# Output weights kept by column halves, one half tile of the projection moved ahead, and one weight piece asked for at its end

## The reference

```
u = rmsnorm(x); z = u @ w_in
a = pooling mixer(z[:, :512]); s = bidirectional S5 scan + GLU(z[:, 512:])
h = x + concat([a, s]) @ w_out
v = rmsnorm(h)
h = h + MoE(v)      # top 1 of 4 groups, then top 2 of its 8 experts, 32 experts of 1024 x 256 (gate, up, down)
h = h + sigmoid(rmsnorm(h) @ W_g + b_g) * (p @ W_ple)
out = rmsnorm(h)
```

## Time and profile before

| what | before |
|---|---|
| median of 3 runs | 522.41 us (522.15 to 522.5) |
| profiled execution, span from first to last instruction | 522.6 us |
| TensorE matmul busy | 484.2 us, 93% |
| VectorE, ScalarE, GpSimd busy | 238.9, 163.6, 161.0 us |
| DMA, mean over the span | 281 GB/s, 146.83 MB |

### The profile page before, as it was taken

The page is one execution under the profiler, slowest core; times in us unless marked ns, Lnnn a source line. Parts: engine busy times, 40 slices in busy tenths (PEclk is TensorE's granted clock), DMA queues, the critical chain, the costliest instruction groups (busy, mean ns, idle before and its releaser), DMA issues.

```text
span 522.6 us, 7298 instructions
## 1 busy us (share of the span) xinstructions
PE 484.2 (93%) x2744; PEld 273.3 (52%) x2744; DVE 238.9 (46%) x683; ACT 163.6 (31%) x265; POOL 161.0 (31%) x144
## 2 busy tenths in 40 slices
PE   3799999999999998999999999779999998899993
PEld 3446776634854476765555554435454544444441
DVE  2899987999233347653222222102211211474524
ACT  5643335456442344111111111002212121313464
POOL 1069999944100111132222222202120210003350
PEclk9999999999999989999999999879999998999998
DMA  8874200499289965999999999999999997970012
GB/s 298 141 204 88 62 0 2 159 129 208 108 360 422 415 249 192 407 412 423 418 415 419 417 419 409 423 416 421 418 420 420 419 409 296 345 312 0 0 80 80
DMA packets 57083, 146.83 MB, mean 281 GB/s; under 512 B 27602, under 2 KB 32758, under 8 KB 44248
## 3 DMA queue, kind: packets, MB, share of 16 engines
q1 hardware_dynamic: 50872, 133.92, 69.0%
q0 software_dynamic: 5904, 12.41, 6.1%
q10 hardware_dynamic: 272, 0.04, 0.0%
HBM read 138.17 MB, written 16.29 MB: 296 GB/s over the span
## 4 chain that ended last, share of the span: by engine, by line
PE 70%; DMA 18%; DVE 3%; ACT 3%; SPq 3%; issue 1%; DVEq 0%
PE bank L1586 65%; DMA h<-in_exp_w_up_dram 11%; DMA big<-in_exp_w_up_dram 6%; SPq L356 3%; DMA h<-in_x_dram 1%; PE bank L1935 1%; PE bank L1677 1%; PE bank L1954 1%; ACT L539 1%; ACT moe L531 1%; PE bank L1821 1%; PE bank L2052 1%; DVE ring L855 1%; DVE moe L1092 1%; DVE moe L855 1%
## 5 line engine op out<-in xcount | busy, mean ns | idle before, releaser
L1586 PE MATMUL bank<-ring,moe 128*64 128x256 f32 (+3 forms) x976 | 127.3, 385 | 3.4 <-DMA ring<-in_exp_w_up_dram 3.0
L1586 PEld LDWEIGHTS bank<-ring,moe 128*64 128x64 f32 (+1 forms) x976 | 76.2, 144 | 38.2 <-issue 15.3
L1512 POOL DMA_INDIRECT pairs_d<-moe,sidx_all x32 | 32.0, 1000 | 159.8 <-PE bank L1935 83.0
L855 DVE TENSOR_TENSOR vrow<-moe,bank 64x128 f32<-64x128 f32 x64 | 18.6, 291 | 125.5 <-ACT moe L754 120.6
L1586 PE MATMUL bank<-big,ut 128*128 128x512 f32 x128 | 58.2, 609 | 1.2 <-ACT ut L676 1.2
L1586 PE MATMUL bank<-ut,big 128*128 128x512 f32 x128 | 57.3, 596 | 1.8 <-ACT ut L543 1.8
L754 ACT ACTIVATE moe<-bank 64x256 f32<-64x256 f32 x32 | 12.1, 378 | 143.3 <-PE bank L1586 143.3
L1586 PE MATMUL bank<-ring,ut 128*128 128x512 f32 x128 | 55.7, 593 | 0.4 <-DVE ut L855 0.4
L531 ACT ACTIVATE moe<-bank 128x512 f32<-128x512 f32 x56 | 32.6, 598 | 59.8 <-PE bank L1586 49.3
L1586 PE MATMUL bank<-big,moe 128*64 128x256 f32 (+1 forms) x264 | 44.9, 455 | 6.6 <-DMA big<-in_exp_w_up_dram 5.7
L1586 PEld LDWEIGHTS bank<-big,ut 128*128 128x128 f32 x128 | 24.6, 196 | 32.0 <-issue 31.7
(11 more groups left out here) (193 smaller groups left out, 600.5 us busy)
## 6 DMA issues: line engine op xcount, KB each, us to landing
ring<-in_exp_w_up_dram SPq DMA_DIRECT2D x19, 1024.0 KB
ring<-in_exp_w_down_dram SPq DMA_DIRECT2D x18, 1024.0 KB
ring<-in_exp_w_gate_dram SPq DMA_DIRECT2D x17, 1024.0 KB
big<-in_exp_w_gate_dram SPq DMA_DIRECT2D x7, 1024.0 KB
big<-in_exp_w_down_dram SPq DMA_DIRECT2D x7, 1024.0 KB
big<-in_exp_w_up_dram SPq DMA_DIRECT2D x6, 1024.0 KB
ut<-in_exp_w_gate_dram SPq DMA_DIRECT2D x4, 1024.0 KB
h<-in_exp_w_up_dram SPq DMA_DIRECT2D x4, 1024.0 KB
```

Of the source, the lines that this page charges most:

```text
L855: return dve.tensor_tensor(o, a, b, op)
L1512: pool.indirect_dma_start(pairs, bass.IndirectOffsetOnAxis(ap=index, axis=0), at(moe, ALL, M_Y + k * 512, [[1, 512]]), None, bounds_check= ...
L1586: return pe.matmul(o, a, b, start=start, stop=stop, skip_group_check=loose)
```

## The change

w_out's rows 512 to 1023 are loaded by two DMAs, one for each half of the columns, each into one piece's place; the matmuls of `wout` read chunk c at `4 * DM + half * PIECE + (c - 4) * 512`. On TensorE `wout1(6)` moves from behind the logits of tiles 1 and 2 to a place ahead of tile 2's transposes, and on VectorE `residual(6)` moves from the middle of the routing arithmetic to a place ahead of tile 2's scaling. Since the add of half tile 6 no longer stands behind the reading of tile 1's logits, TensorE gets a wait of its own (`logit_sb`) ahead of the last tile's transposes, which go into the bank that held them. SyncE asks for piece 14 after seven half tiles, in place of eight; pieces 15 and 21 still wait for eight.

```diff
             sp.wait_ge(zp_ps, NB)
-            sp.dma_start(at(big, ALL, 4 * DM, [[DM, 4], [1, DM]]),
-                         dr(A["w_out"], 4 * P * DM, [[DM, P], [P * DM, 4], [1, DM]])).then_inc(ld_wout1, 16)
+            for half in range(2):
+                sp.dma_start(at(big, ALL, 4 * DM + half * PIECE, [[512, 4], [1, 512]]),
+                             dr(A["w_out"], 4 * P * DM + half * 512, [[DM, P], [P * DM, 4], [1, 512]])
+                             ).then_inc(ld_wout1, 16)
...
+            sp.wait_ge(wo1_ps, 2 * NT - 1)
+            weights(sp, 14)
             sp.wait_ge(wo1_ps, 2 * NT)
-            for p in (14, 15, 21):
+            for p in (15, 21):
                 weights(sp, p)
...
             logits(0)
+            residual(6)
             turned(2)
             norm(2)
             logits(1)
...
             first_best("sel", "m1", "q1", "q2", "oh1")
-            residual(6)
             seq(pick(qv("s2", eight), qv("oh1", eight), -3.0e38, qv("sel", eight), ALU.mult, ALU.add))
...
+                    w = c * DM + half * 512 if c < 4 else 4 * DM + half * PIECE + (c - 4) * 512
                     last = mm(bank[dst][:, :], at(ut, ALL, c * T + t * P, [[1, P]]),
-                              at(big, ALL, c * DM + half * 512, [[1, 512]]), c == chunks[0], c == chunks[-1])
+                              at(big, ALL, w, [[1, 512]]), c == chunks[0], c == chunks[-1])
...
-            pe.wait_ge(ld_wout1, 16)
+            pe.wait_ge(ld_wout1, 32)
...
             logits(0)
+            wout1(6)
             turned(2)
             logits(1)
             logits(2)
-            wout1(6)
             wout1(7)
+            pe.wait_ge(logit_sb, 2)
             turned(NA)
             logits(NA)
```

## The result

The change made the kernel slower: 524.92 us median of 8 runs (523.99 to 526.72) against 522.45 us (522.03 to 524.05, 8 runs), a ratio of 1.0037 with an interval of 1.0019 to 1.0055. The forecast was 520.4 us, with a range of 518.8 to 522.8 and a chance of 0.12 for slower.

What follows compares the result with a forecast made beforehand. Expert-weight transfers were taken to bound the kernel, with standstills before 304.8 us costing time at the end. The least of 2.5, 2.35 and 2.1 us, said as 2.0, off 522.41 gave 520.4 us, range 518.8 to 522.8.

Steps and rivals of the forecast that it cites:

- Step 3, d: VectorE's routing arithmetic and add of half tile 7: the whole routing chain comes 0.67 us later, the change's cost.
- Step 7, c: Experts' releases: pieces 24 to 26 have a lead of 2.8 us, so 2.1 us of gain stays after the delay.
- step 4: TensorE's clock may fall in `wout1(7)`, which then ends at 200.7, before VectorE's 201.36, so the chain does not move.
- slower: TensorE in the last tile's chain, 200.5 to 213 us: clock falls cost 1.7 us each, two give 523.7; chance 0.12.
- what bounds the kernel: Weight stream: a standstill before 304.8 us costs as much at the end; TensorE or VectorE time there costs nothing by itself.
- list of leads: Queue's stock over its next issue: 0.5 us for pieces 18 and 19, 2.8 for 24 to 26, 3.3 for the next.
- Step 2, a: SyncE's piece 14, issued at 190.95, moves before or in the dead stretch; at most 2.5 us leave the later queue.
- Step 6, b: Last h store lands earlier, pieces 18 and 19 go out at 209.65; the queue can be 2.35 us ahead without a gap.
- The lag of 1.0 us: Weight queue: 1.0 us from a DMA's issue to its first bytes; the forecast's own range allowed 1.0 to 1.7.
- Steps 1 and 5: Column halves of w_out cost nothing; tile 2's later scaling and store and the `logit_sb` wait make nothing wait.
- Hidden anyway: Weight queue: the gap only moves from 195 to behind 206 us, time stays about 522.3; chance 0.26.
- More than the piece: Last expert on TensorE: its clock stays up, saving some 1.6 us more, 518.8 us; chance 0.12.

Runs made afterwards that it cites:

- g0: The changed kernel run again with no edit; 524.79 us, one run.
- e4: The changed kernel with piece 14 asked for together with 15 and 21 again, so only the new order and halves remain; 525.22 us, ratio 1.0036.
- e1: The changed kernel with two 512-column matmuls of constants put into TensorE's wait for the masks; 523.88 us, ratio 1.0011 to the kernel before.
- g2: The changed kernel with two filler matmuls ahead of `rank(0)` and piece 18 early as well; 524.11 us, ratio 1.0014 to the kernel before.
- e3: The kernel before with column halves and piece 14 after seven half tiles, in the old order; 522.38 us, ratio 0.9991.
- e2: The kernel before with w_out's second half loaded by column halves and nothing else; 522.69 us, ratio 0.9988.
- g1: The kernel before with column halves and pieces 14 and 18 early, old order, second run of this edit; 523.69 us, ratio 1.0004.
- g3: The kernel before with column halves and piece 14 after seven half tiles, old order, second run of this edit; 523.17 us, ratio 0.9993.
- f1: The kernel before with two 512-column matmuls of constants ahead of `rank(0)`, a delay of 1.7 us; 523.78 us, ratio 1.0012.
- f2: The kernel before with four 512-column matmuls of constants ahead of `rank(0)`, a delay of 3.4 us; 525.15 us, ratio 1.0023.
- f0: The kernel before run once more, unedited, for a second profile; 522.58 us, one run.
- f3: The kernel before with column halves and pieces 14 and 18 early, old order, first run of this edit; 522.9 us, ratio 0.9978.

## Why the prediction was wrong

Two steps failed: step 3 priced the delay of the routing chain at 0.67 us, where it is 2.2, and step 7 took 2.8 us of such a delay to be free, where much less is. A fall of TensorE's clock, which step 4 and the rival "slower" had seen coming, came on top in after.

**Step 3, d: failed.** The working set the new order (201.36, measured 201.44) against 200.69 of the profile of before. That 200.69 holds a clock fall which six of the nine profiles of the old order don't have. The fall makes VectorE wait 2.21 us for half tile 6 in the middle of its arithmetic, and the forecast took wait and add together, 197.93 less 195.16 = 2.77 us, as what the move removes. Without a fall they are 0.58 and 0.61 (195.33 to 195.94), 1.2 us. Removing 1.2 from a delay of 3.44 leaves 2.2, as the table has it. The absolute times were right; the base was an execution of about 524.4 us that was set equal to a median of 522.41. Its span of 522.6, so near the median, hid this. By itself this step doesn't turn the sign: with d = 2.2 the forecast's own sum still has c = 2.8 - 2.2 = 0.6 us of gain.

**Step 4 and the rival "slower": the place was right, the weight too small.** In g0 the fall came in `wout1(7)`, where step 4 puts it, and there it is free. In after and e4 it came behind the wait for the masks, at the place that the rival names: 1.65 us in the chain of after (26.69 less 25.04), against its 1.7, and next to nothing in e4. e1 has neither the wait nor a fall, and is 1.3 us faster than e4. All three profiles of the new order without added matmuls have a fall somewhere, and three of the nine of the old; that is too few to say that the order makes falls more frequent. By the Trainium skill (TensorE: Matmul & The Clock Gate, HAM oscillation) falls follow idle gaps of TensorE. The traces agree in part only: with the gap filled the clock was up in e1 and g2, but at 192 it falls in some executions and in others not, with TensorE busy in all. The rival asked for two falls to turn the sign. With d = 2.2 and one fall, 3.9 us, the sum gives c = -1.1: a loss of 1.1 us, where 1.9 were measured (1.0037, 1.0 to 2.9).

**Step 7, c, and "what bounds the kernel": failed.** The step took a delay of the experts' releases to be free up to 2.8 us. The cleanest case against it has no delay at all: e3 was 2.2 us ahead and had lost all but 0.6 of it by 244 us, in part at the very issue with the lead of 2.8 (below). Of the delays, e1 and g2 have 2.2 us and no fall. e1's ratio is 0.0023 above e2's, 1.2 us; g2's is 0.0010 and 0.0021 above those of g1 and g3, 0.5 and 1.1 us. f1 and f2, with 1.7 and 3.4 us, are 0.6 and 1.2 us above the kernel before. The last expert's start says more: 1.5 and 1.6 us for e1 and g2, counted from tile 2's store and against f0. So between a quarter and three quarters of these 2.2 us reach the end, and the size of the lead is known only roughly: above nothing by f2's time, under 2.8 us by e1 and e3. The premise that TensorE's time ahead of 304.8 costs nothing by itself holds only for what the queue's stock covers, and that was overrated.

**What the list of leads leaves out.** Pieces 16 and 17 wait for the first picked rows, and 22 and 23 for an expert, so they hang on the same chain; the forecast has a lead for 18 and 19 and for 24 to 26, and none for these four. In after 16 and 17 go out at 215.74 us, 1.6 later than before (214.15), and the window from 216 to 217 moves 90 GB/s. From 208 to 226 us after's stream moves 326 GB/s and e3's 379, 1.0 MB or 2.3 us apart (after's whole stretch runs 0.6 us later than e3's, which is part of it), mostly before pieces 24 to 26 are asked for:

```profile
208.00:226.00 18.00, 16.62 (x135) 11.90 (x133) 12.59 (x48) 3.72 (x9) 3.58 (x4) 1.00 0.96 379
```

**Step 2, a: right in time, wrong in worth.** The piece filled the dead stretch (300 GB/s in 192 to 195 in after; 0.9 MB, 2.2 us, ahead of e2 at 208 us in e3). Then it was given back at two places. Windows of e3, and of g3 from 226 on microsecond by microsecond:

```profile
209.00:212.00 3.00, 3.00 (x28) 2.73 (x28) 2.27 (x7) 1.04 (x2) 0.00 (x0) 1.00 0.76 258
226.00:229.00 3.00, 2.56 (x24) 1.96 (x24) 1.06 (x2) 0.01 (x1) 1.87 (x3) 1.00 0.82 294
229.00:240.00 11.00, 11.00 (x84) 6.19 (x81) 3.04 (x8) 1.95 (x4) 3.33 (x5) 1.00 1.01 418
```

```profile
226.00:227.00 1.00, 0.96 (x8) 0.85 (x8) 0.71 (x5) 0.84 (x3) 0.53 (x1) 1.00 1.02 414
227.00:228.00 1.00, 0.56 (x6) 0.40 (x6) 1.00 (x2) 0.00 (x0) 0.31 (x1) 1.00 1.09 283
228.00:229.00 1.00, 1.00 (x13) 0.81 (x10) 0.01 (x1) 0.00 (x0) 0.73 (x1) 1.00 0.79 328
```

The same windows of e2 read 385, 419 and 416 GB/s. At 244 us e3 is 0.6 us ahead of e2 (cumulative MB of such windows from 184 us on, by 418 GB/s) and g3 0.7, and both stay 0.6 to 0.8 ahead to 432; f0, without an early piece, is 0.0 to 0.2 ahead by the same count, so a tenth or two mean nothing here. 0.6 is the measured least of a, b and c in the old order, where the forecast's terms with d = 0 give 2.35. Its share in the end is lost in the spread: the last expert of g3 starts at e2's distance from the first.

**Step 6, b: as forecast for the issue, in part by luck** (209.46 for 209.65; the store landed in 7.0 us where it took 9.8). The step took one piece's 2.5 us off for one piece less in the queue. e3 and g3 have one less as well, and their store took 8.9 and 9.4 us. And even so the queue ran nearly dry for two microseconds, 104 GB/s in 209 to 211: the lead of 0.5 us was none.

**The lag of 1.0 us**, on which all leads rest, was read from first bytes. In g3 pieces 24 to 26 go out at 224.66 and traffic still dips from 227 on, 2.3 us later; in e2, at 224.37, with the stock that a later piece 14 leaves, it doesn't. First bytes flowed after 1.0 us; full rate took longer, 2.3 us and more here, if the dip is the end of the older stock, which no run separates. Against this stands g0, which issued at 228.07 and shows no window under 340 GB/s from 216 on to 240; so the lag isn't one number, and what sets it stays open. Why after's stream runs at 376 GB/s in 231 to 240, at a DMA share of 1.00, is open too.

**Steps 1 and 5: right.** Halves alone 0.9988; nothing waited for the moved scaling, stores or `logit_sb`.

**"Hidden anyway": right for the piece alone** (e3 0.9991, g3 0.9993), but the order it was bought with cost 2.5 us. **"More than the piece"**: the last expert ran at full clock in after, e1 and e4 and not in g0 and g2, and gave its 1.7 us (7.08 against 5.39). So the new order is slower in spite of it. Why the clock was up there stays open.

Nothing was found that is faster: the old order with early pieces (0.9991 and 0.9993 with 14, 0.9978 and 1.0004 with 14 and 18) can't be told from the kernel before.

## What to carry to other kernels

Before a time is taken from one profile as the base of a sum, compare its span with the spans of other executions, and look for a clock fall or a long wait in the very stretch that the change touches: what a reordering "removes" may be a disturbance that most executions lack. Work moved ahead of the head of a dependency chain delays it by its full length, less only the waiting that it fills in the usual execution. A queue's slack is only good for what it is ahead at full rate, not at first bytes, and the list of its slacks has to hold every issue that the delayed chain lets out. Before chain time is spent on early loads, delay the chain on purpose by a known amount and see how much of it reaches the end.

## What the runs showed of the hardware that was not expected

- The clock falls to 0.50 for some 3 to 7 us behind the same instructions in some executions and not in others, with the program unchanged: `wout1(6)` and (7) took 8.76 us in one profile of the kernel before and 7.11 in the next. Of five profiles of the new order three had a fall, each at another place or of another length (197 to 200; 203 to 206; 203 to 210).
- Two 512-column matmuls (1.88 us) whose results nobody reads, put in place of a wait of 1.87 us, went with a clock at 1.00 in both kernels that had them in the new order, and with 1.2 to 1.4 us less time than after. These are one profile of each.
- With weights in the hardware queue, the store of h's last tile on the software queue took 6.4 to 9.8 us (e1 and before), against 3.8 for one alone. The store of tile 2 shows the same: 3.8 us in before, 7.6 to 8.9 in f3, g1 and g2, where piece 18 is in the queue beside it. The Trainium skill (DMA: Bandwidth & Descriptors, Queues, rings and completion order) has a DMA engine take turns between its queues by packets; with equal turns the 0.52 MB would move in some 2.5 us at half of 418 GB/s (an estimate), and these rows don't show that.
